# Second layer's gate and output panels as seven half-size products, with the context tiles normalised later and the front reordered

## The chip, the cores and the metric

The kernel is one program on one NeuronCore of a Trainium2 chip. The metric is device time in microseconds (us), as the median of several executions. Everything is computed in 32-bit floats. The engines are TensorE (PE in the profile, with its weight loads as PEld), VectorE (DVE), ScalarE (ACT), GpSimd (POOL) and SyncE (SP, which issues the weight transfers).

## The reference, cut to what matters

A sequence of 256 latent and 256 context tokens of width 2048 goes through two transformer layers and a third, hybrid layer. The change lies in layer 1 (the second), in which only the latent tokens are still updated, in the step into the third layer, and at two other places (the first 60 us, and the start of the last merge).

```python
# layer l = 1: no context output
u = h @ o_w_in[i];  uc = hc @ o_w_in[i]          # h, hc: normalised latent and context rows
...
y = jnp.concatenate([y1, y2], axis=-1) * jax.nn.silu(ug)      # ug: the gate, 2048 columns, latent rows only
x = x + gate * (y @ w_o[l])                                    # 2048 x 2048, latent rows only
...
# the third layer reads both:  x_ctx is an input of its own (ctx_2)
h_lat = rms_norm(x_lat, norm_g) * (1 + scale_l[:, None]) + shift_l[:, None]
h_ctx = rms_norm(x_ctx, norm_g) * (1 + scale_c) + shift_c
h = jnp.concatenate([h_ctx, h_lat], axis=1)
q (latent), k, v (both) = parts of h @ w_in
```

## The kernel before, in words

**Panels.** Every weight matrix is cut into panels of 256 columns, stored in two halves of 1 MB ("low": the first 1024 rows, "top": the rest). A panel is fetched by SP as two transfers into a slot. The list `ring` fixes by hand the order in which SP fetches and PE uses the panels; modulation panels (`mod`) are woven in between. SP walks this list strictly in order: before each half it waits until the slot's last user has let go of it, and everything behind waits with it. `fetch` (L952) holds these waits. In the second layer the order is gate1 4, mod, gate1 5, mod, gate1 6, mod, gate1 7, wo1 0, mod, wo1 1, mod, wo1 2 to wo1 7, mod, n_q 0. All of these alternate between the two slots of `w`.

**Plain panels.** `project` (L1148) multiplies a panel directly. For latent rows alone (`cml`: gate1, wo1, n_q) a panel is two passes of 16 matmuls with 256 moving columns. Each f32 matmul shows in the trace as two MATMUL records (so 32 for a pass). A pass ends in one of two PSUM banks; ACT and DVE take it out while the next pass runs.

**Fast panels.** Some panels are done as seven products of half-size blocks instead of eight (Winograd's form): a11·b11, s2·t2, s3·t3, s1·t1, a12·b21, a22·t4, s4·b22. PE runs them in this order in `product` (L1561, matmul L1610). The four sums s of the weights (`sums`, L2800, adds at L2809 to L2815) are made by DVE for each panel; the four sums t of the activations (`tee`, L2786, adds at L2790 to L2796) once for each set of panels. The results are put together by ACT (`keep_first`, `first_quarter`) and by DVE (`common` at L2833 and L2835, then `fourth`, `third`, `second`). In `product`, the second product waits for both kinds of sums, the fifth for `keep_first`, the sixth for `common`, the seventh for `fourth`.

DVE works through one fast panel in this order (L2865):

```python
            def fast_panel(F, after):
                ahead = sums(after) if after is not None else iter(())
                next(ahead, None)          # waits until the NEXT panel has landed, first of its four adds
                if mod_before(F.kind, F.j) is not None:
                    mod_add(mod_before(F.kind, F.j))
                next(ahead, None)          # second add
                common(F)
                ...
```

Before the change the fast panels are a_qk 3 to 7, a_v, gate0 5 to 7, wo0 1 to 7, n_k, n_v 0 and 1, and all 56 panels of the final merge (mg, br, out).

**Modulation panels.** `mod_rows` (L1113, matmul L1126) is 32 records on PE after the panel in front of it; it waits for its transfer and for the `mod_add` of the modulation panel before.

**From layer 1 to the third layer.** After attention d, PE runs gate1 4 to 7, then wo1. The second context input is loaded into `x_context` by POOL (L1026, 2 MB) once the first pass of gate1 4 is done; ACT waits for it (`s_x2`) ahead of gate1 4's tanh and squares it during gate1 4 to 7. The context tiles of `h` are normalised by DVE (`h_tile(2, t, 1, lrc)`) and shifted by ACT during wo1. After wo1 the latent tiles are normalised, PE starts n_q (eight passes, which read latent tiles alone), and DVE makes the sums t of all 512 rows (`tee(h0_parts, ...)`, after waiting for `s_hc` and `s_hl`: every shift of every tile) and the sums s of n_k 0. n_k reads the context tiles too.

**The front.** The first 130 us alternate modulation panels 0 to 15 with the first two a_qk panels, tile by tile (`front_tile`, L1632), as tiles of `h` come out.

**The merge.** For each j, DVE runs sums for the next mg panel, `common` of this one, sums of the br panel, and so on; ACT takes the first product of br 0 only after the last quarter of mg 0.

Of the kernel before, what the change touches and what calls it, by code (L numbers as in the profile page):

```python
# [252 lines left out]
def build(nc, A, out):  # L253
# [4 lines left out]
    with ctx:  # L258
# [60 lines left out]
        lrc = z(1536, NL)  # L319
# [536 lines left out]
        def add_ring_fast(name, j, sums, b, t, dst, work, same, sums_used):  # L856
# [4 lines left out]
                     blocks(low_slots[g], 8, 2, P), blocks(top_slots[g], 8, 2, P), sums, b, t, (0, 1, 2, 3), NL, dst, work,  # L861
# [23 lines left out]
        for n in range(10):  # L885
# [5 lines left out]
                          next_work[n % 2], f - 1, f - 2 if n >= 2 else None)  # L891
        n_work = [[z(WK + 2560 + 256 * (3 * b + n), 256) for n in range(3)] for b in range(2)]
# [45 lines left out]
        def _(sp):  # L938
# [13 lines left out]
            def fetch(at, src, kt):  # L952
# [10 lines left out]
                sp.dma_start(low_slots[b][:, 0:n], src[:, 0:n]).then_inc(s_wlow[b], 16)  # L963
                if used > 0:
# [38 lines left out]
        def _(pool):  # L1003
            loads = [(cond, A["cond"], s_first), (sel, A["c_sel"], s_small), (bmod, A["bmod"], s_small), (ng, A["ng"], s_small),
                     (mats[:, 0:3, :], A["c_mat"], s_small), (rope, A["c_rope"], s_const),
                     (hg, A["hg"], s_const), (dg, A["dg"], s_const), (rwp, A["rwp"], s_const)]
# [82 lines left out]
        def _(pe):  # L1089
# [58 lines left out]
            def project(name, js=None, layer=None, gates=None):  # L1148
# [3 lines left out]
                for j in js if js is not None else range(s.n):  # L1152
# [3 lines left out]
                    for n in range(s.nt):  # L1156
# [4 lines left out]
                        for i in range(2 if s.kind == "tm" else 1):  # L1161
                            for k in range(s.kt):
# [11 lines left out]
                                elif first and gates == "gate1" and k in (0, KT - 2, KT - 1):  # L1174
                                    g = pass_no[gates, 7, 0] + {0: -1, KT - 2: 0, KT - 1: 1}[k]
                                    pe.wait_ge(s_evac[g % 2], g // 2 + 1)
                                    if k == 0:
                                        pe.wait_ge(s_evac[(g - 1) % 2], (g - 1) // 2 + 1)
# [17 lines left out]
                        if n == s.nt - 1 and mod_after(name, j) is not None and (name, j) != ("wo1", 7):  # L1196
# [364 lines left out]
            def product(F, n):  # L1561
# [14 lines left out]
                elif n == 1:  # L1576
                    if F.n_sum is None:
                        pe.wait_ge(s_sum0, 1)
                        pe.wait_ge(s_th, 4)
# [4 lines left out]
                    if F.kind == "gate0" and F.j == 5:  # L1584
                        pe.wait_ge(s_th, 2)
                    if F.kind == "n_k" and F.j == 0:
                        pe.wait_ge(s_th, 3)
                    if F.kind == "wo0" and F.j == 1:
                        pe.wait_ge(s_ty, 1)
                    if F.kind == "br" and F.j < 3:  # L1590
                        pe.wait_ge(s_ty, F.j + 2)
# [24 lines left out]
            def fast_panel(name, j, between=lambda n: None):  # L1616
# [7 lines left out]
                if mod_after(name, j) is not None and (name, j) != ("wo0", 7):  # L1624
# [7 lines left out]
            def front_tile(k, cs=range(4)):  # L1632

                if k == 0:
                    for b in (7, 8):
                        pe.wait_ge(s_wlow[b], 16)
                        pe.wait_ge(s_wtop[b], 16)
# [8 lines left out]
            pe.wait_ge(s_cond, 1)  # L1646
            mod_rows(0)
            pe.wait_ge(s_small, 64)
            pe.wait_ge(s_lsu, 14)
            for e in range(2):  # L1650
                for n in range(2):
                    last = mm(ps[:, 4 + e, 0:NL], ones, facc[e][:, n * NL:(n + 1) * NL], start=(n == 0), stop=(n == 1))
            last.then_inc(s_fsum, 1)
# [81 lines left out]
            run(project("gate1", range(4, 8)))  # L1735
            value = project("wo1", gates="gate1")
# [5 lines left out]
            run(value)  # L1742
            pe.wait_ge(s_lacc, 14 + 7 + 14)
# [75 lines left out]
        def _(act):  # L1819
# [39 lines left out]
            def residual_squares(name, sums, parts, js=range(8)):  # L1859

                s = segs[name]
                for t in range(2 * js[0], 2 * js[-1] + 2):
# [14 lines left out]
                    if n == 1 and mod_after(name, j) is not None and (name, j) != ("wo1", 7):  # L1877
# [222 lines left out]
            def first_quarter(F):  # L2100
# [4 lines left out]
                if F.kind == "wo0" and F.j >= 2:  # L2105
                    act.wait_ge(s_xr, 2 * F.j - 2)
                if F.kind == "mg" and F.j >= 3:
# [3 lines left out]
                if F.kind == "out":  # L2111
                    act.wait_ge(s_md, min(23 + F.j, 24))
                    if F.j >= 2:
                        act.wait_ge(s_xr, 14 + 2 * F.j - 2)
# [38 lines left out]
            for m in range(16):  # L2153
# [5 lines left out]
                mod_copy(m)  # L2159
                if m == 0:  # L2160
                    layer_root(1, 0, 512)
            for p in FIRST_TILES[15]:
# [140 lines left out]
            act.wait_ge(s_x2, 16)  # L2303
            value = gate_tanh("gate1", range(4, 8))
            for n in range(8):
                next(value)
                if n >= 3:
                    act.wait_ge(s_lacc, 14 + n - 2)
                f(lacc2 if n == 0 else lsq2[:, n % 2, :], xcf[:, 512 * n:512 * (n + 1)], ACT.Square).then_inc(s_lsq, 1)
            run(value)  # L2310
            for t, _ in enumerate(residual_squares("wo1", (14 + 7, 2), [(xl, False), (xl, True)])):
                if t == 0:
                    layer_root(3, 0, NL, lrc)
                if 2 <= t <= 9:
                    for tile in (2 * t - 4, 2 * t - 3):
                        shift(2, tile, 1, e)
                        e += 1
# [6 lines left out]
            run(take("n_q"))  # L2324
# [879 lines left out]
```

## Time and profile before

| | |
|---|---|
| median of 3 runs | 3682.98 us (3677.32 to 3685.85) |
| the profiled execution's own time | 3685.7 us |
| its span, first to last instruction | 3683.9 us |
| mean granted TensorE clock | 0.995 |
| busy share: PE / PEld / DVE / ACT / POOL | 97% / 75% / 44% / 19% / 5% |
| HBM, mean over the span | 132 GB/s |

Start times in the trace count from the span's start. In a timeline the columns are start, length, engine, source line, operation, output<-input, partitions x elements and count; square brackets give the idle time of the engine just before and what ended it. A matmul's length includes the drain of its last record, so PE's pace is read from start to start.

### The profile page before, as it was taken

The page shows a single profiled execution, that of the slowest core. Times are in us where ns is not written, and L with a number is a line of the kernel's source. Part 1 is how long each engine was busy: PE and PEld are TensorE (multiplying, and loading weights), DVE is VectorE, ACT ScalarE, POOL GpSimd, SP SyncE. Part 2 cuts the span into 40 slices and gives each one's busy share as a digit, 9 for nine tenths or more (in the row PEclk, how much of TensorE's full clock was granted, in tenths as well). Part 3 has the DMA queues.
Part 4 walks back from the last instruction along what each step waited for, and adds up shares of the span by engine and source line. Part 5 has one row for each costly group of instructions (what it writes and reads, how often), then busy time and mean ns, then how long its engine had stood idle before and what let it go on. Part 6 is the DMA issues. An engine that isn't in the chain of part 4 may idle for free. (4 is left out here: it accounts for less than half of the span.)

```text
span 3683.9 us, 68776 instructions
## 1 busy us (share of the span) xinstructions
PE 3591.5 (97%) x30368; PEld 2751.7 (75%) x30368; DVE 1613.1 (44%) x3143; ACT 716.9 (19%) x1677; POOL 188.9 (5%) x265
## 2 busy tenths in 40 slices
PE   6999999999999999999999999999999999999998
PEld 3589646557787666778888675677777687999998
DVE  3324355553343422212421623455555554666565
ACT  2101143320002223211100311222222221000000
POOL 0000000000000000000000000122222211000000
PEclk9999999999999999999999999999999999999999
DMA  9443322334443433465443242111111122444443
GB/s 402 184 183 138 115 92 92 107 115 168 183 160 137 181 122 110 162 239 182 179 164 149 81 138 92 40 44 41 49 50 49 48 71 104 161 164 169 172 172 115
DMA packets 73514, 490.08 MB, mean 133 GB/s; under 512 B 8449, under 2 KB 10497, under 8 KB 19457
## 3 DMA queue, kind: packets, MB, share of 16 engines
q1 hardware_dynamic: 70848, 466.65, 34.4%
q0 software_dynamic: 2368, 19.02, 1.4%
q8 instruction: 241, 3.95, 0.4%
q14 instruction: 57, 0.46, 0.0%
HBM read 481.44 MB, written 4.19 MB: 132 GB/s over the span
## 5 line engine op out<-in xcount | busy, mean ns | idle before, releaser
L1188 PE MATMUL ps<-h,w 128*128 128x256 f32 (+1 forms) x2240 | 733.2, 467 | 5.9 <-ACT h L1890 5.4
L1188 PEld LDWEIGHTS ps<-h,w 128*128 128x128 f32 x2240 | 407.5, 191 | 192.1 <-issue 160.9
L1296 PE MATMUL ps<-h,w 128*128 128x256 f32 (+1 forms) x1024 | 374.8, 500 | 1.3 <-issue 1.3
L1296 PEld LDWEIGHTS ps<-h,w 128*128 128x128 f32 x1024 | 180.6, 189 | 89.0 <-issue 69.3
L1610 PE MATMUL ps<-h,zone 128*128 128x128 f32 (+1 forms) x1360 | 187.8, 291 | 0.8 <-DVE y L2853 0.8
L1465 PE MATMUL ps<-zone 64*64 64x64 f32 x4608 | 178.1, 219 | 5.8 <-issue 5.5
L1610 PEld LDWEIGHTS ps<-h,zone 128*128 128x128 f32 x1360 | 173.8, 192 | 7.5 <-issue 1.2
L1465 PEld LDWEIGHTS ps<-zone 64*64 64x64 f32 x4608 | 161.1, 134 | 9.5 <-issue 7.5
L1053 POOL TENSOR_TENSOR zone<-zone 128x256 f32<-128x256 f32 x160 | 130.4, 828 | 672.8 <-ACT zone L2035 506.0
L1610 PE MATMUL ps<-zone 128*128 128x128 f32 (+1 forms) x960 | 154.3, 310 | 0.0
L1126 PE MATMUL ps<-w,zone 128*32 128x256 f32 x2048 | 127.4, 390 | 25.6 <-DMA w<-in_wm 21.2
L2698 DVE TENSOR_TENSOR zone<-zone,ps 128x512 f32<-128x512 f32 (+1 forms) x160 | 101.0, 634 | 112.0 <-PE ps L1465 111.4
L1610 PEld LDWEIGHTS ps<-zone 128*128 128x128 f32 x960 | 136.8, 191 | 7.9
L1188 PE MATMUL ps<-y,w 128*128 128x256 f32 (+1 forms) x576 | 139.6, 403 | 0.0
L1610 PE MATMUL ps<-h,w 128*128 128x128 f32 (+1 forms) x976 | 139.2, 298 | 0.0
L1610 PE MATMUL ps<-y,w 128*128 128x128 f32 (+1 forms) x880 | 136.9, 302 | 1.2 <-ACT zone L2093 1.2
L1610 PEld LDWEIGHTS ps<-h,w 128*128 128x128 f32 x976 | 127.8, 192 | 7.2 <-issue 2.1
L1188 PEld LDWEIGHTS ps<-y,w 128*128 128x128 f32 x576 | 109.0, 190 | 28.6 <-issue 15.6
L1610 PEld LDWEIGHTS ps<-y,w 128*128 128x128 f32 x880 | 121.8, 191 | 8.1 <-ACT zone L2093 1.6
L1126 PEld LDWEIGHTS ps<-w,zone 128*32 128x32 f32 x2048 | 60.7, 111 | 89.0 <-issue 47.6
L1949 ACT ACTIVATE zone<-ps,st 128x512 f32<-128x512 f32 (+1 forms) x112 | 66.2, 594 | 281.3 <-PE ps L1256 241.8
L1610 PE MATMUL ps<-y,zone 128*128 128x256 f32 (+1 forms) x656 | 118.1, 331 | 2.0 <-DVE y L2796 2.0
(466 smaller groups left out, 5428.8 us busy)
## 6 DMA issues: line engine op xcount, KB each, us to landing
w<-in_wm SPq DMA_DIRECT2D x128, 1024.0 KB, 6.8
w<-in_w SPq DMA_DIRECT2D x40, 1024.0 KB, 5.0
w<-in_we SPq DMA_DIRECT2D x34, 1024.0 KB, 5.3
w<-in_wi SPq DMA_DIRECT2D x34, 1024.0 KB, 5.0
w<-in_wrw SPq DMA_DIRECT2D x32, 1024.0 KB, 5.0
w<-in_wo SPq DMA_DIRECT2D x24, 1024.0 KB, 5.3
x_context<-in_wmg SPq DMA_DIRECT2D x24, 1024.0 KB, 6.6
w<-in_wbr SPq DMA_DIRECT2D x48, 512.0 KB, 4.7
```

The source lines that it names most:

```text
L1053: tt(am[:, n % 8, :, :, :].rearrange("p h d t -> p h (d t)"), dsb[:, :, n % 4, :, :].rearrange("p h d t -> p h (d t)"), lvm[:, n // 4:n // ...
L1126: last = mm(ps[32 * g:32 * g + 32, 7, 0:COLS], cond32[:, k, :], halves.rows(k), start=(k < 4), stop=(k >= KT - 4))
L1188: last = mm(pass_psum(s, q), rows[:, n * P:(n + 1) * P], src[k], start=(k == 0), stop=(k == s.kt - 1))
L1296: last = mm(ps[:, m, 0:T - NC * n], halves.rows(k)[:, m * P:(m + 1) * P], h[:, k, NC * n:T], start=(k == 0), stop=(k == KT - 1))
L1465: last = mm(ps[r, 5 + m % 2, at:at + 64], xt if x else mine, mine if x else xt, start=True, stop=True)
L1610: last = mm(ps[:, F.banks[bank], 0:F.cols], left[:, k, :], right[:, k, :], start=(n < 4 and k == 0), stop=(k == F.hk - 1), skip_group_chec ...
L1949: last = f(e_b[:, g % 2, si, 0:u.nk], src, ACT.Exp, bias=st[:, g % 2, 2 + si:3 + si], scale=1.0 if u.mask is not None else u.scale, accum_ ...
L2698: v_.tensor_tensor(v, v, ps[:, 5 + n % 2, :].rearrange("p (x t) -> p x t", x=2)[:, x, :], ALU.add)\
```

## The change

- gate1 5 to 7 and wo1 1 to 7 become fast panels (ten), with 128 instead of 256 moving columns, since they have latent rows alone. gate1 5, gate1 7 and the odd wo1 panels go into a third slot (6, in the free half of `y`); gate1 6 and the even wo1 panels into the slot of gate1 4; the modulation panels among them all go into the other slot of `w`.
- n_v 2 becomes a fast panel too (`N_FAST` 3).
- The tanh and the gate product of gate1 5 to 7, and the residual of wo1 1 to 7, work on whole panels; ACT's wait for the second context comes after gate1 5's tanh.
- The context tiles are normalised after the latent ones, at the start of n_q, and ACT shifts them between the passes of n_q: three after each of passes 2 to 6, the last after pass 7.
- Front: the top halves of a_qk 0 and 1 are fetched after modulation panel 3; POOL's loads of the constants that are needed later wait for the first eight tiles; the halves of the squares' sums are added on DVE, and the norm's sum, root and reciprocal come ahead of modulation panel 0's steps.
- Merge: for j = 0, `common` and `fourth` of mg 0 come first on DVE, then the sums t for br 0.

```diff
-        N_FAST = 2
+        N_FAST = 3
...
-                or name == "n_k" or (name == "n_v" and j < N_FAST)
+                or name == "n_k" or (name == "n_v" and j < N_FAST) or (name == "gate1" and j >= 5) or (name == "wo1" and j >= 1)
...
+            elif (name == "gate1" and j in (5, 7)) or (name == "wo1" and j % 2 == 1):
+                b = 6
+            elif (name == "gate1" and j == 6) or name == "wo1":
+                b = ring_slot[place["gate1", 4]]
+            elif name == "mod" and place["gate1", 5] < at < place["n_q", 0]:
+                b = 1 - ring_slot[place["gate1", 4]]
...
+        g1_sums = [blocks(z(2048 + 1024 * n, 1024), 8, P) for n in range(4)]
+        y1_parts = quarters(y256, 8)
...
+            add_ring_fast(name, j, next_bufs[n % 2], h_parts if name == "gate1" else y1_parts, g1_sums,
+                          [v[:, P * c:P * c + P] for c in range(4)], g1_work[n % 2], f - 1, f - 2 if n >= 2 else None, P)
...
             # SP, after the fetch of each modulation panel
+                    if j == 3:
+                        s = segs["a_qk"]
+                        for p in range(2):
+                            sp.dma_start(top_slots[7 + p], s.dram[s.panel(p), :, 2048:4096]).then_inc(s_wtop[7 + p], 16)
...
             # POOL
+            pool.wait_ge(s_hs, 8)
+            for dst, src in ((rope, A["c_rope"]), (hg, A["hg"]), (dg, A["dg"]), (rwp, A["rwp"])):
+                pool.dma_start(dst[tuple(slice(None) for _ in dst.shape)], src).then_inc(s_const, 16)
...
             # PE, front
+            pe.wait_ge(s_lsu, 16)
+            for e in range(2):
+                last = mm(ps[:, 4 + e, 0:NL], ones, facc[e][:, 0:NL], start=True, stop=True)
+            last.then_inc(s_fsum, 1)
             mod_rows(0)
...
             # PE, layer 1
-            run(project("gate1", range(4, 8)))
-            value = project("wo1", gates="gate1")
+            run(project("gate1", [4]))
+            evacuated(passes_to("gate1"))
+            for j in range(5, 8):
+                fast_panel("gate1", j)
+            quarters_taken(by_panel["gate1", 7])
+            value = project("wo1", [0], gates="gate1")
...
             run(value)
+            evacuated(passes_to("wo1"))
+            for j in range(1, 8):
+                fast_panel("wo1", j)
+            quarters_taken(by_panel["wo1", 7])
             pe.wait_ge(s_lacc, 14 + 7 + 14)
...
             # ACT, n_q
-            run(take("n_q"))
+            value = take("n_q")
+            for p in range(8):
+                next(value)
+                if p >= 2:
+                    for t in range(3 * p - 6, min(3 * p - 3, KT)):
+                        shift(2, t, 1, e)
+                        e += 1
+            run(value)
...
             # DVE, layer 1
+            run(tee(h_parts, g1_sums, done=s_th))
+            run(sums(by_panel["gate1", 5]))
+            run(gate("gate1", y256, [4]))
+            for j, squares in ((5, (1, 2)), (6, (3, 4, 5)), (7, (6, 7))):
+                F = by_panel["gate1", j]
+                fast_panel(F, by_panel["gate1", j + 1] if j < 7 else None)
+                dve.wait_ge(s_gtanh, 3 + j - 4)
...
+            for j in range(1, 8):
+                F = by_panel["wo1", j]
+                fast_panel(F, by_panel["wo1", j + 1] if j < 7 else None)
...
             last.then_inc(s_x1, 1)
+            for t in range(KT):
+                h_tile(2, t, 1, lrc)
             dve.wait_ge(s_hc, 3 * KT)
             dve.wait_ge(s_hl, 3 * KT)
             run(tee(h0_parts, h0_sums, done=s_th))
...
             # DVE, merge
+                if j == 0:
+                    common(F)
+                    fourth(F)
+                    run(tee(y_parts[0], y_sums[0], done=s_ty))
+                    run(sums(B))
+                    next(ahead)
+                    next(ahead)
```

## Rows read from the trace of the kernel before

**Rows 1.** Page, busy us (share of the span) and instructions of each engine.
```profile
PE 3591.5 (97%) x30368; PEld 2751.7 (75%) x30368; DVE 1613.1 (44%) x3143; ACT 716.9 (19%) x1677; POOL 188.9 (5%) x265
```

**Rows 2.** Timeline of PE, gate1 5 to the start of n_q.
```profile
1578.93 3.49 PE L1126 MATMUL ps<-w,zone 128*32 128x256 f32 x32 [4.47 <-DVE modc L2400]
1582.35 7.17 PE L1188 MATMUL ps<-h,w 128*128 128x256 f32 x32
...
1598.54 7.14 PE L1188 MATMUL ps<-h,w 128*128 128x256 f32 x32
...
1668.70 76.14 PE L1188 MATMUL ps<-y,w 128*128 128x256 f32 x352
1746.02 1.13 PE L1744 MATMUL ps<-zone,mats 128*128 128x512 f32 x2 [1.18 <-DVE zone L2573]
```

**Rows 3.** Timeline of PE, first and sixth product of a merge panel.
```profile
3133.32 1.95 PE L1610 MATMUL ps<-h,zone 128*128 128x128 f32 x16
...
3142.25 1.95 PE L1610 MATMUL ps<-h,zone 128*128 128x128 f32 x16
```

**Rows 4.** Timeline of all engines, a fast n_k panel behind a modulation panel.
```profile
1863.27 3.72 PE L1610 MATMUL ps<-h,x_latent 128*128 128x256 f32 x16
...
1864.25 0.55 SPq L966 DMA_DIRECT2D w<-in_w  x1
...
1875.06 1.22 DVE L2809 TENSOR_TENSOR zone<-w 128x1024 f32<-128x1024 f32 x1 [13.12 <-DMA w<-in_w]
...
1878.32 0.42 DVE L2835 TENSOR_TENSOR zone<-ps,zone 128x256 f32<-128x256 f32 x1
```

**Rows 5.** Timeline of all engines, n_q and the start of n_k.
```profile
1770.19 2.28 DVE L2790 TENSOR_TENSOR y<-h 128x2048 f32<-128x2048 f32 x1
...
1777.04 2.28 DVE L2796 TENSOR_TENSOR y<-h,y 128x2048 f32<-128x2048 f32 x1
...
1792.41 1.23 DVE L2809 TENSOR_TENSOR zone<-x_latent 128x1024 f32<-128x1024 f32 x1 [13.08 <-DMA x_latent<-in_w]
...
1796.07 1.22 DVE L2815 TENSOR_TENSOR zone<-x_latent,zone 128x1024 f32<-128x1024 f32 x1
...
1810.13 0.39 ACT L1836 ACTIVATE zone<-ps 128x256 f32<-128x256 f32 x1 [6.52 <-PE ps L1188]
...
1814.14 1.03 PE L1610 MATMUL ps<-y,zone 128*128 128x256 f32 x4
```

**Rows 6.** Timeline of PE, n_v 1 (fast), n_v 2 (plain), n_v 3.
```profile
1943.47 3.84 PE L1607 MATMUL ps<-w,h 128*128 128x128 f32 x32
...
1970.77 14.08 PE L1182 MATMUL ps<-x_latent,h 128*128 128x256 f32 x64
...
2000.67 2.64 PE L1182 MATMUL ps<-w,h 128*128 128x256 f32 x11
```

**Rows 7.** Timeline of all engines at the end of gate1 4.
```profile
1567.89 0.53 POOL L1026 DMA_DIRECT2D x_context<-in_ctx  x1 [172.50 <-PE ps L1188]
...
1577.71 0.42 DVE L2548 SCALAR_TENSOR_TENSOR zone<-zone,ps 128x256 f32<-128x256 f32 x1 [18.02 <-ACT zone L1849]
```

**Rows 8.** DMA of the windows 1862:1890, 1968:1992 and 0:60 (KB each, median us to landing).
```profile
w<-in_wm SPq DMA_DIRECT2D x4, 1024.0 KB, 5.9
...
w<-in_wm SPq DMA_DIRECT2D x2, 1024.0 KB, 14.4
...
DMA packets 3295, 23.49 MB, mean 391 GB/s; under 512 B 544, under 2 KB 544, under 8 KB 816
```

**Rows 9.** Windows, PE alone: us, busy (records), granted clock, DMA share, GB/s.
```profile
1580.00:1585.00 5.00, 5.00 (x39) 0.79 0.64 206
3120.00:3124.00 4.00, 3.20 (x27) 1.00 0.35 147
```

**Rows 10.** Timeline of PE at the end of wo0 and in mg 0.
```profile
1145.08 1.90 PE L1700 MATMUL ps<-zone,mats 128*128 128x512 f32 x2 [3.79 <-DVE zone L2977]
...
3119.85 2.05 PE L1610 MATMUL ps<-h,x_context 128*128 128x128 f32 x16 [3.04 <-DVE zone L2835]
```

More of the change, by code:

```diff
@@ L854, in add_fast, with add_ring_fast @@
             by_panel[kind, j] = fasts[-1]
-        def add_ring_fast(name, j, sums, b, t, dst, work, same, sums_used):
+        def add_ring_fast(name, j, sums, b, t, dst, work, same, sums_used, cols=NL):
             at = place[name, j]
@@ L1195, in project @@
                             mod_cols(mod_before(name, j))
-                        if n == s.nt - 1 and mod_after(name, j) is not None and (name, j) != ("wo1", 7):
+                        if n == s.nt - 1 and mod_after(name, j) is not None:
                             mod_rows(mod_after(name, j))
@@ L1585, in product @@
                         pe.wait_ge(s_th, 2)
+                    if F.kind == "gate1" and F.j == 5:
+                        pe.wait_ge(s_th, 3)
+                    if F.kind == "wo1" and F.j == 1:
+                        pe.wait_ge(s_ty, 2)
                     if F.kind == "n_k" and F.j == 0:
-                        pe.wait_ge(s_th, 3)
+                        pe.wait_ge(s_th, 4)
                     if F.kind == "wo0" and F.j == 1:
@@ L1623, in fast_panel @@
                     between(n)
-                if mod_after(name, j) is not None and (name, j) != ("wo0", 7):
+                if mod_after(name, j) is not None and (name, j) not in (("wo0", 7), ("wo1", 7)):
                     mod_rows(mod_after(name, j))
@@ L1646, in _ @@
             pe.wait_ge(s_cond, 1)
-            mod_rows(0)
[L1648 to L1653, printed above, removed]
+            pe.wait_ge(s_small, 64)
+            pe.wait_ge(s_lsu, 16)
+            for e in range(2):
+                last = mm(ps[:, 4 + e, 0:NL], ones, facc[e][:, 0:NL], start=True, stop=True)
+            last.then_inc(s_fsum, 1)
+            mod_rows(0)
             mod_cols(0)
@@ L1876, in residual_squares @@
                     last.then_inc(s_lsq, 1)
-                    if n == 1 and mod_after(name, j) is not None and (name, j) != ("wo1", 7):
+                    if n == 1 and mod_after(name, j) is not None:
                         mod_copy(mod_after(name, j))
@@ L2106, in first_quarter @@
                     act.wait_ge(s_xr, 2 * F.j - 2)
+                if F.kind == "gate1" and F.j >= 6:
+                    act.wait_ge(s_gy, 3 + F.j - 5)
+                if F.kind == "wo1" and F.j >= 2:
+                    act.wait_ge(s_xr, 14 + 2 * F.j - 2)
                 if F.kind == "mg" and F.j >= 3:
@@ L2302, in _, with second_squares @@
             attend("d", beside("d", gate_tanh))
[L2303 to L2311, printed above, removed]
+            run(gate_tanh("gate1", [4]))
+            for j, squares in ((5, range(0, 3)), (6, range(3, 6)), (7, range(6, 8))):
+                F = by_panel["gate1", j]
+                keep_first(F)
+                first_quarter(F)
+                copy_after("gate1", j)
+                act.wait_ge(s_c12, F.f + 1)
+                act.wait_ge(s_c11, F.f + 1)
+                f(g1_t, g1_c, ACT.Tanh, scale=0.5).then_inc(s_gtanh, 1)
+                if j == 5:
+                    act.wait_ge(s_x2, 16)
+                for n in squares:
+                    if n >= 3:
+                        act.wait_ge(s_lacc, 14 + n - 2)
+                    f(lacc2 if n == 0 else lsq2[:, n % 2, :], xcf[:, 512 * n:512 * (n + 1)], ACT.Square).then_inc(s_lsq, 1)
+            for t, _ in enumerate(residual_squares("wo1", (14 + 7, 2), [(xl, False), (xl, True)], [0])):
                 if t == 0:
                     layer_root(3, 0, NL, lrc)
[L2314 to L2317, printed above, removed]
+            def second_squares(j):
+                for t in (2 * j, 2 * j + 1):
+                    act.wait_ge(s_xr, 14 + t - 1)
+                    if t >= 3:
+                        act.wait_ge(s_lacc, 14 + 7 + t - 2)
+                    f(lsq[:, t % 2, 0:NL], xl[:, t, :], ACT.Square)
+                    f(lsq[:, t % 2, NL:T], xl[:, t, :], ACT.Square, scale=ng[:, t, 3:4]).then_inc(s_lsq, 1)
+            for j in range(1, 8):
+                F = by_panel["wo1", j]
+                keep_first(F)
+                if j >= 2:
+                    second_squares(j - 1)
+                first_quarter(F)
+                if j < 7:
+                    copy_after("wo1", j)
+            second_squares(7)
             layer_root(5, 0, NL, lr2)
@@ L2844, in fourth @@
                     dve.wait_ge(s_xr, 2 * F.j - 2)
+                if F.kind == "gate1" and F.j >= 6:
+                    dve.wait_ge(s_gy, 3 + F.j - 5)
+                if F.kind == "wo1" and F.j >= 2:
+                    dve.wait_ge(s_xr, 14 + 2 * F.j - 2)
                 if F.kind == "mg" and F.j >= 3:
@@ L3124, in _ @@
             rw_readout(7)
-            run(tee(y_parts[0], y_sums[0], done=s_ty))
             late = tee(m_parts, m_sums, rows=slice(6, 8), done=s_tm)
@@ L3134, in _ @@
                 ahead = sums(mgs[j + 1] if j < 23 else outs[0])
-                next(ahead)
-                next(ahead)
-                common(F)
-                run(sums(B))
-                fourth(F)
+                if j == 0:
[5 more added lines that the diff above has]
+                    next(ahead)
+                else:
+                    next(ahead)
+                    next(ahead)
+                    common(F)
+                    run(sums(B))
+                    fourth(F)
                 next(ahead)
```

87 lines of the change are left out of this document (53 added, 34 removed).

## The prediction, made before the changed kernel was run

> **What bounds the kernel now.** I read the page first: PE is busy for 97% of the span and no other engine for more than 44% (PEld runs underneath) [rows 1]. So a change pays only by taking work off PE, and costs whatever makes PE wait. Next the timeline of PE through the stage that is changed: plain panels run end to end there, and the only idle times are the 4.47 us ahead of the modulation rows behind gate1 4, and 1.18 us ahead of the sums at the end of wo1 [rows 2]. Then I looked at stages that already do what the change spreads: the merge for the pace of half-size products with 128 columns [rows 3], n_k for a fast panel that has a modulation panel in front [rows 4, 5], n_v for both forms of the same panel [rows 6]. Last the DMA views, since new slots change what is fetched when [rows 7, 8].
>
> **What it takes off PE.** A plain panel is 64 records; 352 records take 76.1 us, so 13.8 us a panel [rows 2]. As a fast panel: five products lie between 3133.32 and 3142.25, 1.786 us each, so seven take 12.5 us [rows 3]. The gain is 1.3 us a panel, 13.0 us for ten. n_v 1 (fast, with its modulation rows) takes 27.3 us from start to start and n_v 2 (plain) 29.9 us [rows 6], so n_v 2 gives 2.6 us. Together -15.6 us. That presumes that everything else stays hidden behind PE, and a shorter panel hides less.
>
> **Fetches behind a modulation panel.** This is the largest cost. SP fetches strictly in ring order. In gate1 5 the next panel, gate1 6, has a modulation panel ahead of it in the queue, and this one waits until the modulation rows just before gate1 5 have let go of its slot. So four halves of 1 MB start to move only when gate1 5 itself starts. n_k is in exactly this position before the change: first product at 1863.27, last of the four halves issued at 1864.25, first add on the landed panel at 1875.06, after 13.12 us of idle time that the transfer ended, and the end of `common` at 1878.32 + 0.42 = 1878.74 [rows 4]. That is 15.5 us after the first product. DVE does it in this order because the first add for the next panel stands ahead of `common` in `fast_panel`. In n_k it costs nothing: five products of 256 columns take over 17 us. Now the sixth product, which waits for `common`, is due after five products of 1.786 us and 0.2 us of modulation columns, 9.1 us. With slightly shorter adds (128 columns) I put `common` at 15.2 us, so PE waits 6.1 us. It happens three times: in gate1 5, gate1 6 and wo1 1, whose next panels all have a modulation panel ahead of them. gate1 7 has only a plain panel behind it, and wo1 2 to 6 have no modulation panels: there the next panel's last half goes out at the sixth product of the panel before and lands some 3 us into this one, in time. Three waits make 18.3 us, give or take 1.5 us each.
>
> **The clock after a wait.** PE idle for 4.47 us was followed by a window with a granted clock of 0.79, part of it at 1.2 GHz, and the modulation rows in it took 3.42 us from start to start [rows 2, 9]. Idle for 3.04 us in the merge, PE kept 2.4 GHz: 1.00 in the window after it [rows 9, 10]. The new waits are longer than both, so I charge each what the 4.47 us cost: 5 us at 0.79 lose 1.05 us, and with the part before 1580 about 1.6 us. Three times: 4.8 us; nothing at the least. The Trainium skill, page "TensorE: Matmul & The Clock Gate", section on HAM oscillation, says that a kernel whose products for one tile are shorter than the wait for the next tile's transfer is throttled again before every tile and pays each time. By that rule all four new waits (these and the one before n_k) are charged, as I do; by the 3.04 us row alone none is, and the sum would be 6.4 us lower.
>
> **From gate1 4 to gate1 5.** The old 4.47 us of idle time were ACT's wait for the second context, which POOL sends for at 1567.89 and which landed just before DVE's 1577.71 [rows 2, 7]. ACT no longer waits there. But DVE now makes gate1 5's four weight sums before it gates gate1 4, and the modulation rows wait for the `mod_add` behind that gate. gate1 5's halves can go out right behind the modulation panel ahead of them, about 1561 (gate1 4's first pass, 7 us, ends when POOL sends). If nothing is in their way they land 10.8 us later, as in n_k [rows 4], at 1572. The context load overlaps them: a modulation panel beside a load by POOL took 14.4 us instead of 5.9 [rows 8]. I take 1577.5, when the context is in. Sums take 4.9 us (1792.41 to 1797.29 [rows 5]), gate and `mod_add` 1.2 us (1577.71 to 1578.93), so the modulation rows start at 1583.6 instead of 1578.93: +4.7 us, and -0.8 us at the other end. The Trainium skill, page "DMA: Bandwidth & Descriptors", section on queues and rings, says that each DMA engine takes turns between its queues by the packet. By that the panel is held back until about the context's end, as the 14.4 us agree; with a first-come queue the sum would be 5.5 us lower.
>
> **Ends of the two runs of fast panels.** After gate1 7 PE waits for the last quarters, 0.5 us. After wo1 7, correction, residuals, squares and sum follow the last product where only the last tile's did: wo0's end, already of this kind, shows 3.79 us of idle time [rows 10] against 1.18 [rows 2]. With half the columns I take +1.6 us, between 0 and 2.6.
>
> **Context tiles in n_q.** The sums t for n_k wait for the shift of every tile. The last context tile is now shifted after the last pass of n_q: copy at 1810.13 + 0.39, shift 0.5, 1811.0. In the trace these four adds ran from 1770.19 to 1779.32, 9.1 us, and n_k 0's weight sums 4.9 us, all hidden under n_q [rows 5]. Now they begin at 1811.0 and end at 1825.0, while n_k's second product, which needs them, is due at 1814.14. PE waits 10.9 us, and 1.6 us more for the clock. The 16 normalising adds themselves are hidden in n_q. I see no bound far from this, since both the wait and the order stand in the code.
>
> **Front.** 23.5 MB move in the first 60 us at 391 GB/s [rows 8], so PE follows the transfers. Putting a_qk's top halves after modulation panel 3 only changes the order of what must have landed by panel 4; POOL's 0.7 MB that are put off are worth 1.8 us at that rate and come back later. I take -1.3 us (-1.8 to 0). The earlier root and reciprocal take no part: the transfers come later.
>
> **Merge.** The 3.04 us wait in mg 0 [rows 10] goes, since `common` is early. But br 0's fifth product needs ACT, which waits for mg 0's last quarter, which DVE reaches only after the same adds as before. I take +0.5 us for the short wait of `fourth` for its product; the bounds are -3.0 and +1.0.
>
> **Sum.** -15.6 + 18.3 + 4.8 + 4.7 + 0.5 + 1.6 + 10.9 + 1.6 - 1.3 + 0.5 = +26.0 us on the profiled execution's 3685.7 us, 3711.7. That execution lies 2.7 us above the median of the runs shown, 3682.98, so I predict 3709 us.
>
> **Rivals.** (1) The fetches are hidden: the next panel lands in time because its slot is free and SP runs ahead. That saves the three waits with their clock, 23.1 us, and leaves +2.9 us: 3686, not slower by what can be told. It decides if the panel lands within 5.7 us of the first product (9.1 less the 3.4 us from landing to `common`). For it: the slot of gate1 4 is free early. Against it: 11.8 us in n_k [rows 4], and the modulation panel ahead in the queue. (2) The sums before n_k are hidden (they run ahead of the last shift): -12.5 us, 3696.5. Against it: the wait for all shifts stands first. (3) Both are hidden, and the first context wait simply goes: -12.5 - 23.1 - 4.7 with -1.3 more for the ends, so 3667 us, the gain that the products alone promise. For it: PE's share of 97%.
>
> **How the numbers follow.** My forecast has 0.80, rival (1) 0.07, (2) 0.07, (3) 0.06. 0.2% (7.4 us) is about what a measurement of this kernel can tell from no change. Slower: 0.80 + 0.07 = 0.87; same 0.07; faster 0.06. The range takes the forecast's bounds: without the context sharing (-5.5), the clock (-6.4) and with the best merge (-3.5) it would be 3693.6; with longer fetches (3 x 1.5) and the worst ends and front (+2.8) it is 3716. So 3693 to 3717, which also holds rival (2).
>
> **What would show it.** In gate1 5, gate1 6 and wo1 1 the sixth product should start about 15 us after the first, with some 6 us of idle time that DVE's `common` ends, and DVE idle until a transfer lands. A lower granted clock should follow. wo1 2 to 6 should take 12.5 us each. n_k 0's second product should wait about 11 us, with DVE's adds of 2048 columns beginning only after n_q's last copy. If instead these products run end to end, or the panel lands within 6 us, the prediction is wrong. So it is if the adds for n_k start inside n_q.

## The result, and the profile after

| | before | after |
|---|---|---|
| median | 3682.05 us (4 runs) | 3710.76 us (4 runs, 3708.86 to 3713.49) |
| ratio, with its 95% interval | | 1.0077 [1.0065, 1.0089] |
| profiled execution's own time, span | 3685.7, 3683.9 us | 3709.6, 3707.8 us |
| mean granted TensorE clock | 0.995 | 0.989 |
| PE busy | 3591.5 us | 3585.1 us |

The change made the kernel 28.7 us slower. PE has 6.4 us less busy time [rows 1], but the span grew by 23.9 us: part of what the products saved went into matmuls at a lower clock, and more than all of it into waits. Where it went is read by taking the start of the first matmul of each stage in both traces (us; "the merge" counts from the last sum of the stage before it, "the last matmul" is the first of the sums at the very end; the last column holds the terms of the prediction's sum that belong to the stage):

| stage, on PE | before | after | difference | predicted |
|---|---|---|---|---|
| start to gate1 4 | 1560.16 | 1556.58 | -3.6 | -1.3 |
| gate1 4 to the first product of gate1 5 | 22.19 | 25.93 | +3.7 | +4.7 |
| gate1 5 to the sums at the end of wo1 | 163.67 | 179.00 | +15.3 | +12.2 |
| those sums, the modulation rows, n_q | 64.59 | 65.94 | +1.4 | 0 |
| n_k and n_v, to attention n | 218.87 | 228.19 | +9.3 | +9.9 |
| attention n to the merge | 1079.49 | 1073.93 | -5.6 | 0 |
| merge to the last matmul | 561.37 | 564.34 | +3.0 | +0.5 |

In the lines below, L1639 is the matmul of a product; L2877, L2879, L2881 and L2883 are the four adds of `sums`; L2858 to L2864 those of `tee`; L2901 and L2903 `common`; L2930 `third`; L2935 `second`. L1151 are the modulation rows, L2468 the end of a `mod_add`, L2616 the gate product, L1925 ACT's shift, L2128 `keep_first`, L980 and L985 SP's two halves of a panel.

**The three waits for a landing.** Timeline of all engines in gate1 5 of the changed kernel, and below it the two other waits of the kind (gate1 6 and wo1 1):

```profile
1582.51 3.17 PE L1639 MATMUL ps<-h,y 128*128 128x128 f32 x16
...
1583.02 0.43 SPq L980 DMA_DIRECT2D w<-in_wi  x1
1583.49 0.47 SPq L985 DMA_DIRECT2D w<-in_wi  x1
...
1594.42 1.23 DVE L2877 TENSOR_TENSOR zone<-w 128x1024 f32<-128x1024 f32 x1 [14.74 <-DMA w<-in_wi]
...
1597.87 0.29 DVE L2903 TENSOR_TENSOR zone<-ps,zone 128x128 f32<-128x128 f32 x1
...
1598.21 3.78 PE L1639 MATMUL ps<-zone,y 128*128 128x128 f32 x16 [5.17 <-DVE zone L2903]
...
1621.72 3.78 PE L1639 MATMUL ps<-zone,w 128*128 128x128 f32 x16 [6.70 <-DVE zone L2903]
...
1674.83 3.78 PE L1639 MATMUL ps<-zone,y 128*128 128x128 f32 x16 [5.99 <-DVE zone L2903]
```

Read it from the bottom of gate1 5 up. PE's sixth product waits 5.17 us, and `common` ends the wait. DVE had been idle for 14.74 us, which the landing of gate1 6 ended; that add stands ahead of `common`. And gate1 6 landed late because its halves went out at 1583.02 and 1583.49, after gate1 5 had begun. The sixth product comes 15.7 us after the first one. This is n_k's picture [rows 4], with products too short to cover it.

**Where nothing is in the way.** First products of wo1 3, wo1 4 and wo1 7, timeline of PE:

```profile
1695.95 1.95 PE L1639 MATMUL ps<-y 128*128 128x128 f32 x16
...
1708.46 1.95 PE L1639 MATMUL ps<-y,w 128*128 128x128 f32 x16
...
1745.98 1.95 PE L1639 MATMUL ps<-y 128*128 128x128 f32 x16
```

From wo1 3 to wo1 4 are 12.51 us, and from wo1 3 to wo1 7 four times 12.51, against 13.8 for a plain panel [rows 2]: the products are as cheap as they were meant to be.

**Before gate1 5.** Timeline of all engines:

```profile
1564.31 0.53 POOL L1051 DMA_DIRECT2D x_context<-in_ctx  x1 [172.50 <-PE ps L1213]
...
1572.93 1.22 DVE L2877 TENSOR_TENSOR zone<-y 128x1024 f32<-128x1024 f32 x1 [12.03 <-DMA y<-in_wi]
...
1577.73 0.41 DVE L2616 SCALAR_TENSOR_TENSOR zone<-zone,ps 128x256 f32<-128x256 f32 x1
...
1578.94 3.64 PE L1151 MATMUL ps<-w,zone 128*32 128x256 f32 x32 [8.06 <-DVE modc L2468]
```

The old wait of 4.47 us [rows 2] has become one of 8.06 us. ACT is no longer late; DVE takes gate1 5's four adds first (1572.93 to 1577.8), then the gate.

**Before n_k 0's second product.** Timeline of all engines:

```profile
1827.43 2.29 DVE L2858 TENSOR_TENSOR y<-h 128x2048 f32<-128x2048 f32 x1 [34.33 <-ACT h L1925]
...
1840.15 1.22 DVE L2883 TENSOR_TENSOR zone<-x_latent,zone 128x1024 f32<-128x1024 f32 x1
...
1841.42 5.12 PE L1639 MATMUL ps<-y,zone 128*128 128x256 f32 x16 [10.25 <-DVE zone L2883]
```

DVE was idle for 34.33 us until ACT's last shift; then eight adds ran with PE waiting. In the kernel before the same adds lay under n_q [rows 5].

**In the merge.** Timeline of all engines at br 0's fifth product:

```profile
3148.82 0.28 DVE L2935 TENSOR_TENSOR y<-ps,zone 128x128 f32<-128x128 f32 x1
...
3149.57 0.26 ACT L2128 ACTIVATE zone<-ps 128x128 f32<-128x128 f32 x1
...
3149.88 2.08 PE L1639 MATMUL ps<-y,w 128*128 128x128 f32 x8 [5.32 <-ACT zone L2128]
```

The 3.04 us in mg 0 [rows 10] are gone, and 5.32 us have appeared one panel later, behind DVE's `second` of mg 0 and ACT.

**The clock behind the waits.** Windows, PE alone, from the end of each of five waits (gate1 5, gate1 6, wo1 1, n_k 0, br 0), then the modulation rows and the first product of gate1 5 (us, busy (records), granted clock, DMA share, GB/s):

```profile
1598.20:1603.70 5.50, 5.49 (x32) 0.66 0.02 3
...
1621.70:1627.40 5.70, 5.68 (x32) 0.64 0.18 26
...
1674.80:1681.20 6.40, 6.37 (x32) 0.56 0.26 55
...
1841.40:1846.40 5.00, 4.98 (x17) 0.71 0.00 0
...
3149.90:3155.00 5.10, 5.10 (x24) 0.50 0.00 0
...
1578.90:1582.50 3.60, 3.56 (x32) 0.50 0.28 43
1582.50:1586.00 3.50, 3.50 (x25) 0.66 0.92 321
```

Every one of the six waits was followed by a stretch in which part of the matmuls, or all, ran at 1.2 GHz. Where PE need not wait (run 1 below), the sixth and seventh product take 3.67 us to the next modulation rows. Behind the first three waits they take 5.53, 5.71 and 6.43 us, which is 1.9, 2.0 and 2.8 us lost.

**At the end of wo1.** Timeline of PE, and the window behind the wait:

```profile
1761.51 1.21 PE L1779 MATMUL ps<-zone,mats 128*128 128x512 f32 x2 [2.86 <-DVE zone L3132]
```

```profile
1761.50:1764.40 2.90, 2.89 (x8) 0.65 0.00 0
```

The sums wait 2.86 us where they waited 1.18 us before [rows 2], and here too the clock behind the wait is lower.

### The profile page after: what moved, and what is told of

Its sections match the earlier page's. It is cut to its first block and busy times, and to the rows that moved or that the text cites. A ratio compares the mean times of both kernels' runs of the same rounds, so it can differ in the third digit from the quotient of the medians.

```text
span 3707.8 us, 70132 instructions
## 1 busy us (share of the span) xinstructions
PE 3585.1 (97%) x30940; PEld 2765.3 (75%) x30940; DVE 1690.3 (46%) x3246; ACT 719.1 (19%) x1694; POOL 191.0 (5%) x265
## 5 line engine op out<-in xcount | busy, mean ns | idle before, releaser
L1213 PE MATMUL ps<-h,w 128*128 128x256 f32 (+1 forms) x2048 | 690.4, 475 | 4.7 <-ACT h L1925 4.7
L1213 PEld LDWEIGHTS ps<-h,w 128*128 128x128 f32 x2048 | 371.7, 191 | 184.3 <-issue 157.8
L1321 PE MATMUL ps<-h,w 128*128 128x256 f32 (+1 forms) x1024 | 374.8, 500 | 1.3 <-issue 1.3
L1321 PEld LDWEIGHTS ps<-h,w 128*128 128x128 f32 x1024 | 180.6, 189 | 89.0 <-issue 69.3
L1639 PE MATMUL ps<-h,zone 128*128 128x128 f32 (+1 forms) x1408 | 193.9, 291 | 0.0
L1639 PE MATMUL ps<-zone 128*128 128x128 f32 (+1 forms) x1280 | 193.3, 301 | 0.0
L1639 PEld LDWEIGHTS ps<-h,zone 128*128 128x128 f32 x1408 | 179.9, 192 | 6.5 <-issue 1.2
L1490 PE MATMUL ps<-zone 64*64 64x64 f32 x4608 | 178.9, 219 | 2.1 <-issue 1.6
L1639 PEld LDWEIGHTS ps<-zone 128*128 128x128 f32 x1280 | 174.1, 192 | 7.9
L1639 PE MATMUL ps<-y,w 128*128 128x128 f32 (+1 forms) x976 | 149.6, 301 | 6.1 <-ACT zone L2128 6.1
L1639 PE MATMUL ps<-y,zone 128*128 128x128 f32 (+1 forms) x768 | 135.3, 329 | 12.2 <-DVE zone L2883 10.2
L1639 PEld LDWEIGHTS ps<-y,w 128*128 128x128 f32 x976 | 133.8, 193 | 13.4 <-ACT zone L2128 6.5
L1639 PE MATMUL ps<-h,w 128*128 128x128 f32 (+1 forms) x1008 | 143.2, 297 | 0.0
L1151 PE MATMUL ps<-w,zone 128*32 128x256 f32 x2048 | 128.1, 391 | 9.4 <-DVE modc L2468 8.1
L1639 PEld LDWEIGHTS ps<-h,w 128*128 128x128 f32 x1008 | 131.5, 192 | 7.6 <-issue 2.5
L1639 PEld LDWEIGHTS ps<-y,zone 128*128 128x128 f32 x768 | 119.1, 198 | 21.6 <-DVE zone L2883 10.6
L1476 PE MATMUL ps<-zone 64*64 64x64 f32 x2560 | 115.5, 219 | 3.4 <-issue 3.1
L1151 PEld LDWEIGHTS ps<-w,zone 128*32 128x32 f32 x2048 | 60.9, 112 | 73.3 <-issue 29.9
```

Source lines behind the costliest of these rows:

```text
L1151: last = mm(ps[32 * g:32 * g + 32, 7, 0:COLS], cond32[:, k, :], halves.rows(k), start=(k < 4), stop=(k >= KT - 4))
L1213: last = mm(pass_psum(s, q), rows[:, n * P:(n + 1) * P], src[k], start=(k == 0), stop=(k == s.kt - 1))
L1321: last = mm(ps[:, m, 0:T - NC * n], halves.rows(k)[:, m * P:(m + 1) * P], h[:, k, NC * n:T], start=(k == 0), stop=(k == KT - 1))
L1476: last = mm(ps[r, 3 + n % 2, i * 64:i * 64 + 64], am[r, n % 8, i // 2, i % 2, :], xx[r, 1, tok, i // 2, i % 2, :], start=True, stop=True)
L1490: last = mm(ps[r, 5 + m % 2, at:at + 64], xt if x else mine, mine if x else xt, start=True, stop=True)
L1639: last = mm(ps[:, F.banks[bank], 0:F.cols], left[:, k, :], right[:, k, :], start=(n < 4 and k == 0), stop=(k == F.hk - 1), skip_group_chec ...
```

## The experiments

Two sets of four kernels ran, each set on one chip, with the kernel before beside it. The first set changes the changed kernel in one place each. The kernel before had a median of 3678.5 us there, so the changed kernel by its ratio of 1.0077 stood at about 3706.8; differences are taken from that. It did not run beside them, and the interval of its ratio is some 4 us either way, so a difference of a few us from it says little by itself; the profiles carry those.

| kernel | median | kernel before beside it | ratio [95%] |
|---|---|---|---|
| fetch ahead of the modulation panel | 3679.0 | 3678.5 | 1.0004 [0.9995, 1.0013] |
| own panel first on DVE | 3684.8 | 3678.5 | 1.0019 [1.0010, 1.0028] |
| context tiles earlier | 3698.3 | 3678.5 | 1.0054 [1.0042, 1.0067] |
| merge order undone | 3704.8 | 3678.5 | 1.0075 [1.0062, 1.0087] |
| fetch and context | 3667.2 | 3680.0 | 0.9968 [0.9956, 0.9981] |
| ... and gate before sums | 3662.8 | 3680.0 | 0.9956 [0.9944, 0.9969] |
| ... and quarters of mg 0 first | 3654.5 | 3680.0 | 0.9935 [0.9923, 0.9947] |
| kernel before, new front alone | 3678.8 | 3680.0 | 1.0000 [0.9991, 1.0009] |

**1. Fetch ahead of the modulation panel.** The order of use stays; only SP's walk is changed:

```diff
+            fetch_at = list(range(len(ring)))
+            for key in (("gate1", 6), ("gate1", 7), ("wo1", 2)):
+                at = place[key]
+                fetch_at[at - 1:at + 1] = [at, at - 1]
-            for at, (kind, j) in enumerate(ring):
+            for at in fetch_at:
+                kind, j = ring[at]
```

> SP fetches gate1 6, gate1 7 and wo1 2 ahead of the modulation panel that stands in front of each in the queue; nothing else changes. Theory A (the three waits come from the place in SP's queue behind a modulation panel whose slot is still in use): the next panel lands before the sixth product is due, the three waits (5.17, 6.70 and 5.99 us, 17.9 together) and the half-clock stretches behind them (about 2 us each) go, so 3711 - 24 = 3687 us. Theory B (the transfer itself or DVE's own adds are what is late, wherever the fetch stands): the sixth products still start about 15 us after the first ones, 3711 us.

Measured: 27.8 us less than the changed kernel, where A expected 24 and B nothing. In the profiles 26.6 us of it lie between gate1 4's start and the sums behind wo1 (178.4 us against 204.9). Timeline, gate1 5 and the start of gate1 6 in this kernel (lines are 5 further down):

```profile
1570.30 0.33 SPq L985 DMA_DIRECT2D w<-in_wi  x1
...
1579.08 1.23 DVE L2882 TENSOR_TENSOR zone<-w 128x1024 f32<-128x1024 f32 x1
...
1581.46 2.05 PE L1644 MATMUL ps<-h,y 128*128 128x128 f32 x16
...
1590.71 1.95 PE L1644 MATMUL ps<-zone,y 128*128 128x128 f32 x16
...
1594.38 1.93 PE L1156 MATMUL ps<-w,zone 128*32 128x256 f32 x32
...
1596.24 2.05 PE L1644 MATMUL ps<-h,w 128*128 128x128 f32 x16
```

gate1 6 is now on its way before gate1 5 starts, and its first add runs 2.4 us before gate1 5's first product. The sixth product follows 9.25 us after the first, with no wait; the prediction had 9.1 us as its due time. From the modulation rows to the sums at the end of wo1 are 156.0 us, 11.1 less than in the kernel before (167.1). The prediction's terms without the three waits and their clock give -10.9.

**2. Own panel first on DVE.** The fetches stay late; in gate1 5, gate1 6 and wo1 1 DVE no longer puts the next panel's add ahead:

```diff
+                if (F.kind, F.j) in (("gate1", 5), ("gate1", 6), ("wo1", 1)):
+                    mod_add(mod_before(F.kind, F.j))
+                    common(F)
+                    fourth(F)
+                    third(F)
+                    second(F)
+                    run(ahead)
+                    return
```

> The fetches stay where they are; in gate1 5, gate1 6 and wo1 1 DVE finishes its own panel (common, fourth, third, second) before the first add for the next panel. Theory A (common waits only because an add for a panel that has not landed stands ahead of it): no wait at the sixth product; the next panel's sums end 4.9 us after its landing or after the own panel's last quarter, about 17.6 us after the first product, where the second product of the next panel is due at 16.4, so some 1.3 us of wait each and hardly any loss of clock: 3711 - 20 = 3691 us. Theory B (the sixth product waits for the transfer or a bank, not for the order on DVE): 3711 us.

Measured: 22 us less. Timeline at gate1 6's second product, where the cost now lies:

```profile
1597.25 1.22 DVE L2877 TENSOR_TENSOR zone<-w 128x1024 f32<-128x1024 f32 x1
...
1600.91 1.22 DVE L2883 TENSOR_TENSOR zone<-w,zone 128x1024 f32<-128x1024 f32 x1
...
1602.18 2.05 PE L1639 MATMUL ps<-zone 128*128 128x128 f32 x16 [1.11 <-DVE zone L2883]
```

The panel is fetched as late as before (its last half goes out 1.0 us after gate1 5's first product in both kernels), but PE waits 1.11 us at the next panel's sums, 3.3 us for all three, in place of 5 to 7 us each at `common`. So a late landing alone is not the price: the add for a panel that has not landed, ahead of work that is due, is what made it long. Either cure takes most of it, and the earlier fetch takes all.

**3. Context tiles earlier.**

```diff
-                    for t in range(3 * p - 6, min(3 * p - 3, KT)):
+                    for t in range(4 * p - 8, min(4 * p - 4, KT)):
```

> ACT shifts four context tiles behind each of passes 2 to 5 of n_q in place of three behind each of passes 2 to 6 and the last behind pass 7. Theory A (n_k 0's second product waits because the sums of the activations can only begin after the last shift): the sums begin near 1815 us and end near 1829 us with the sums of the weights, the second product is due at 1831, and the wait of 10.25 us goes with about 1.5 us of clock: 3711 - 11.8 = 3699 us. Theory B (DVE's adds or the panel's landing set the start): 3711 us.

Timeline, last shifts and the second product of n_k 0:

```profile
1816.99 2.29 DVE L2858 TENSOR_TENSOR y<-h 128x2048 f32<-128x2048 f32 x1 [21.71 <-ACT h L1925]
...
1829.71 1.22 DVE L2883 TENSOR_TENSOR zone<-x_latent,zone 128x1024 f32<-128x1024 f32 x1
...
1832.81 3.62 PE L1639 MATMUL ps<-y,zone 128*128 128x256 f32 x16
```

The wait is gone, with the adds 1.9 us ahead of it. From n_k's start to attention n are 216.3 us against 228.2 (-11.9, as A has it), and 2.6 less than in the kernel before (218.9): that is n_v 2. The median fell by 8.5 us, which by the 4 us of its reference does not speak against 11.9; in the profile the two waits of gate1 5 and 6 were also 0.9 and 0.4 us longer than in the changed kernel.

**4. Merge order undone.** DVE's order in mg 0 as before the change:

```diff
                 if j == 0:
-                    common(F)
-                    fourth(F)
                     run(tee(y_parts[0], y_sums[0], done=s_ty))
-                    run(sums(B))
-                    next(ahead)
-                    next(ahead)
-                else:
...
```

> Only the order of DVE's work in mg 0 is put back as it was before the change. Theory A (the new order only puts the waits together, and one long wait of 5.3 us before the fifth product of br 0 costs the clock where 3.0 and 0.8 us did not): waits of 3.0, 0.8 and 0.4 us come back, the clock in the 5 us behind them is 1.00 again instead of 0.50, and the merge takes 452.2 us instead of 455.2: 3711 - 3 = 3708 us. Theory B (the merge is longer for another reason, such as the place of its transfers): 3711 us and a merge of 455 us.

Measured: 2 us less, which the timing cannot tell from none. In the profile the merge to the last matmul took 562.6 us, 1.8 less than in the changed kernel. But the reason given was wrong in one half. Timeline of the wait, and the window behind it:

```profile
3137.20 3.78 PE L1639 MATMUL ps<-h,x_context 128*128 128x128 f32 x16 [3.04 <-DVE zone L2903]
```

```profile
3137.10:3142.10 5.00, 4.89 (x23) 0.50 0.31 134
```

The 3.04 us wait is back, and this time the clock behind it was 0.50, where it had been 1.00 in the kernel before [rows 9]. In the kernel of run 8, whose merge is the same code, it was 1.00 again (timeline, then window):

```profile
3111.34 0.82 PE L1618 MATMUL ps<-h,x_context 128*128 128x128 f32 x5 [3.03 <-DVE zone L2841]
```

```profile
3111.20:3116.20 5.00, 4.06 (x34) 1.00 0.31 131
```

So one and the same wait, in the same code of the merge, costs the clock in the profiled execution of one kernel and not in those of two others.

**5. Fetch and context together.** Runs 1 and 3 in one kernel.

> The fetch order of the first run and the earlier shifts of the third together. Theory A (two separate waits on two separate chains): the gains add, 11.9 us off the 3679 us of the first, 3667 us. Theory B (the sums of the activations start earlier but end against n_q's tail anyway, so that a new wait takes the place): no more than 4 us off, 3675 us.

Measured: 3667.2 us, 12.8 less than the kernel before. The gains of 1 and 3 add up, as A has it: run 1 stood 0.5 us above its kernel before, so 13 us came off.

**6. Gate before sums.** Added to run 5:

```diff
-            run(sums(by_panel["gate1", 5]))
             run(gate("gate1", y256, [4]))
+            run(sums(by_panel["gate1", 5]))
```

> The run before it, and DVE gates gate1 4 ahead of the weight sums of gate1 5. Theory A (the modulation rows behind gate1 4 wait for a gate that stands behind four adds): they start near 1572.8 us instead of 1578.9, the second product of gate1 5 waits 1.4 us for its sums, and about 2 us of half clock go: 6.5 us off, 3660.5 us. Theory B (the modulation panel's landing beside the 2 MB of the second context ends that wait, DVE or not): 3667 us.

Timeline, the modulation rows behind gate1 4 and gate1 5's second product, and the window behind it:

```profile
1571.46 1.93 PE L1156 MATMUL ps<-w,zone 128*32 128x256 f32 x32
...
1572.91 1.23 DVE L2882 TENSOR_TENSOR zone<-y 128x1024 f32<-128x1024 f32 x1
...
1577.85 3.50 PE L1644 MATMUL ps<-zone 128*128 128x128 f32 x16 [2.25 <-DVE zone L2888]
```

```profile
1577.80:1583.00 5.20, 5.15 (x31) 0.67 1.01 422
```

The rows start without any wait, 8.1 us earlier than in run 5 (1579.59). The second product then waits 2.25 us for the sums, and n_q starts 6.8 us earlier. The median fell by 4.4 us, with spreads of 7 and 9 us; the direction is A's, and its size is not settled.

**7. Quarters of mg 0 first.** Added to run 6, for j = 0:

```diff
                     run(sums(B))
+                    third(F)
+                    second(F)
                     next(ahead)
                     next(ahead)
+                    common(B)
+                    fourth(B)
+                    run(ahead)
+                    run(tee(y_parts[1], y_sums[1], done=s_ty))
+                    continue
```

> The run before it, and DVE takes the third and second quarter of mg 0 right behind the sums for br 0, ahead of the sums for mg 1 and of the second set of sums of activations. Theory A (br 0's fifth product waits on ACT for mg 0's last quarter, which stands behind adds that are needed later): the wait of 5.3 us and its half clock go, some 0.8 us comes back at mg 1's second product; 6 us off, 3654.5 us. Theory B (those adds are needed as soon as they are made, so that the wait moves to mg 1): no change that can be told, 3660.5 us.

Measured: 3654.5 us, 8.3 less than run 6 and 25.5 less than the kernel before (the ratio is 0.9935); it is the fastest kernel of the study. Timeline, mg 0's last quarter and br 0's fifth product, and the windows:

```profile
3094.20 0.28 DVE L2940 TENSOR_TENSOR y<-ps,zone 128x128 f32<-128x128 f32 x1
...
3097.21 1.06 PE L1644 MATMUL ps<-y,w 128*128 128x128 f32 x8
```

```profile
3086.00:3100.00 14.00, 14.00 (x127) 1.00 0.76 277
3100.00:3110.00 10.00, 10.00 (x92) 1.00 0.42 143
```

`second` comes right behind mg 0's last product, PE is busy all through, and the merge to the last matmul takes 554.9 us, 6.5 less than in the kernel before. The adds that were put back were not needed earlier. One part of the 6.5 us has another source. The second product of the first `out` panel waits just as long in all ten profiles (1.95 or 1.96 us); in eight of them slower products follow, in those of run 1 and run 7 none do. Timeline and window of this place, first in the changed kernel:

```profile
3591.54 3.42 PE L1639 MATMUL ps<-y,zone 128*128 128x128 f32 x16 [1.95 <-DVE y L2864]
```

```profile
3591.50:3595.20 3.70, 3.66 (x19) 0.56 0.83 348
```

and in run 7:

```profile
3536.53 2.02 PE L1644 MATMUL ps<-y,zone 128*128 128x128 f32 x16 [1.95 <-DVE y L2869]
```

```profile
3536.50:3540.20 3.70, 3.67 (x33) 1.00 0.79 326
```

The two products from there take 3.6 us in run 7 and 5.3 us in the kernel before and in run 6, so 1.6 us of the 6.5 come from there and not from the new order.

**8. The front alone**, on the kernel before:

```diff
+                if b in (7, 8):
+                    return
...
+            pool.wait_ge(s_hs, 8)
...
-            pe.wait_ge(s_lsu, 14)
+            pe.wait_ge(s_lsu, 16)
...
```

> The kernel before with the changes to the front alone. Theory A (the front gives 2.5 us, as attention b starts 2.6 us earlier in the changed kernel, and the 6 us that the third layer's scan stage took less in its profile than in that of before are differences between executions): 2.5 us below the kernel before, and the scan stage, whose code is the same, shows 839 to 844 us instead of 849. Theory B (the scan stage is shorter because of what the change does ahead of it): the scan stage shows 849 us. A front that gave nothing would show no difference.

Measured: 1.2 us less, no difference that can be told. In the profile gate1 4 starts 2.9 us earlier than in the kernel before (1557.25 against 1560.16); 2.25 us of it are there when the front ends, and most of the rest comes near 651 us, where the kernel before waited 0.6 us for a weight panel in its profile. The scan stage (the stretch ahead of the merge that took 849.3 us in the kernel before) took 845.1 us. Its code is the same in all kernels; over the nine profiles other than that of the kernel before it took 839.1 to 845.1 us, so 849.3 was the longest of ten. Most of the -5.6 us of the stage table is thus a difference between executions; whether all of it is stays open.

## Why the prediction was right

**The fetches (+18.3).** Measured 5.17 + 6.70 + 5.99 = 17.9 us, at the three places that were named, with `common` as what ended them. Runs 1 and 2 show both links of the chain: the place in SP's queue, and the add ahead of `common`.

**The clock behind them (+4.8).** Mis-sized: 6.7 us. All the new waits were charged, none was free. The 1.6 us each had been taken from the wait of 4.47 us; the products behind the new ones lost 1.9 to 2.8. Behind gate1 4's wait, now 8.06 us, gate1 5's first product took 3.0 us instead of 1.9, which the sum had not. The Trainium skill's rule ("TensorE: Matmul & The Clock Gate", section on HAM oscillation), that each such wait is paid anew in throttled products, agrees with these six windows (0.50 to 0.71). The shorter waits of this case, 1.95 to 3.04 us, went both ways (last section) and settle nothing about it.

**The products (-15.6).** 12.51 us a panel where nothing waited; run 1 gave -11.1 for gate1 and wo1 with their ends against -10.9; n_v 2 gave -2.6.

**gate1 4 to 5 (+4.7).** +3.7. gate1 5 landed at 1572.93. gate1 4 starts 3.6 us earlier than before, so this answers to 1576.5 in the prediction's time: 1.0 us before the 1577.5 of the shared load, and 4.5 us after the 1572 of a transfer alone. The Trainium skill's rule of turns between queues ("DMA: Bandwidth & Descriptors", section on queues and rings) agrees: the panel took 15.3 us from its last issue, against 10.8 alone [rows 4].

**n_k 0 (+12.5).** The wait was 10.25 us, and the second product took 5.0 us to the third's start instead of 3.5: 11.75 us together, and run 3 took 11.9 back.

**The ends (+2.1).** 0.6 us after gate1 7, and a wait of 2.86 us against 1.18 after wo1 7: as predicted. Behind it the sums and the modulation rows took 7.7 us to n_q instead of 6.7, with a granted clock of 0.65 in the 2.9 us after the wait where it had been 1.00; that was not in the sum.

**The front (-1.3).** Probably mis-sized: when the front ends, run 8's profile is 2.25 us ahead of that of the kernel before, outside the bounds of -1.8 to 0; the nine profiles with the new front are 1.6 to 3.0 us ahead, two of them inside the bounds. The old front has a single profile to go by, and in the median the front cannot be told from nothing. The term counted only the transfers put off, by their size; which part of the front gives the rest was not tried.

**The merge (+0.5).** +3.0, outside its bounds. The step was right, that DVE reaches mg 0's last quarter only after the same adds, so that the wait only moves. Missing was that the one wait of 5.32 us is longer than the three before it together (3.04, 0.80 and 0.41 us), and that 5 us at 0.50 follow it.

**The sum** was +26.0 us; the two profiled executions differ by 23.9, the medians by 28.7. The misses (clock and merge one way, front and scan stage the other) nearly cancel, so it is in part luck that the forecast of 3709 us came within 1.8 us of the median. It is not luck that the waits came out at 17.9 us against 18.3, and at 11.75 us against 12.5, at the places that were named. What made the sign was the waits and the clock behind them: run 7 has the same products with most of those waits removed, and is 25.5 us faster than the kernel before.

## What to carry to other kernels

A product that becomes shorter hides less (here three fetches and one set of adds): before speeding up a stage, list what it covers (transfers in queue order, adds, copies) and set each one's time against the new length. Where one queue feeds two kinds of panel in order, put the panel whose slot is free ahead of the one whose slot is still in use, and on an in-order engine never put work on data that has not landed ahead of work that is due (here 22 us for undoing that alone). Moving work to a later, idle place is free only if what waits for its last piece also has room there.

## What the hardware showed that was not expected

The clock behind a wait is not fixed by the wait's length. After idle times of 3.03 and 3.04 us in the same code it was 1.00 in two executions and 0.50 in a third. After 1.95 us ahead of the second product of the first `out` panel it was 0.56 in the changed kernel and 1.00 in run 7. After 2.25 us in run 6 it was 0.67, after 2.86 us at the end of wo1 0.65. Each of the six waits shown for the changed kernel (5.17 to 10.25 us) cost something (0.50 to 0.71 in the window behind), and so a wait of 2 to 3 us has to be priced with both ends, nothing and the loss at 1.2 GHz. What decides it was not tried here.
